# Sixteen slots for expert weights, earlier first loads, a router product with standing weights, and expert results added straight to the residual

## The reference, cut to what matters

```
x = x + g1 * y                                # y: the merged branches through w_o
u = modulate(rmsnorm(x, norm2_g), sh2, sc2)
logits = u @ router_w + router_b              # 256 x 32
top_val, top_idx = top_k(logits, 4); gate = softmax(top_val)
for each expert e, with the tokens that chose it (padded):
    hcat = u[tok] @ w1[e] + b1[e]             # 1024 -> 2048
    h_glu, h_lin = min(hcat[:, :1024], 7), clip(hcat[:, 1024:], -7, 7)
    act = h_glu * sigmoid(1.702 * h_glu) * (h_lin + 1)
    y_tok += gate * (act @ w2[e] + b2[e])     # 1024 -> 1024
x = x + g2 * y;  return rmsnorm(x, final_norm_g)
```

## Time and profile before

| | us |
|---|---|
| median of 3 runs | 2567.33 |
| profiled execution | 2567.04 |
| its span, first to last instruction | 2565.2 |
| first pass starts / last unit of the last pass ends | 1603.91 / 2544.28 |
| TensorE busy | 2408.0 (94%) |
| VectorE busy | 725.1 (28%) |
| ScalarE busy | 410.0 (16%) |
| HBM traffic | 604.65 MB read, 236 GB/s over the span |

### The profile page before, as it was taken

How to read it: one execution, slowest core, us unless ns; L and a number is a source line. 1 busy time by engine, 2 the same in 40 slices (tenths; PEclk the granted TensorE clock), 3 DMA queues, 4 the chain that set the end, 5 groups by cost and what they waited for, 6 DMA issues and landing times.

```text
span 2565.2 us, 32855 instructions
## 1 busy us (share of the span) xinstructions
PE 2408.0 (94%) x13468; PEld 1806.2 (70%) x13468; DVE 725.1 (28%) x1780; ACT 410.0 (16%) x928; POOL 0.2 (0%) x4
## 2 busy tenths in 40 slices
PE   8789998999889998999999898999999999999997
PEld 7678887888778887888876587555555555555554
DVE  6722264120432212000344543112111211111112
ACT  4222101000322102000023412111111111111111
POOL 0000000000000000000000000000000000000000
PEclk9899999999999999999999997999999999999999
DMA  6024475664214442132211054899999999999996
GB/s 248 33 99 152 160 276 189 240 226 170 81 66 140 156 148 115 66 115 91 71 70 49 7 211 184 359 422 421 422 422 422 421 422 421 422 421 422 421 422 261
DMA packets 83842, 606.90 MB, mean 237 GB/s; under 512 B 9328, under 2 KB 9712, under 8 KB 10000
## 3 DMA queue, kind: packets, MB, share of 16 engines
q1 hardware_dynamic: 83760, 605.73, 59.8%
HBM read 604.65 MB, written 1.05 MB: 236 GB/s over the span
## 4 chain that ended last, share of the span: by engine, by line
PE 79%; DMA 10%; DVE 7%; ACT 3%; issue 1%; SPq 0%; ACTq 0%; DVEq 0%
PE bank L521 30%; PE bank L898 13%; DMA spare<-in_experts 9%; PE bank L518 8%; PE bank L576 6%; PE bank L925 6%; PE bank L863 3%; PE bank L535 2%; PE bank L892 2%; DVE arena L1355 2%; PE bank L561 2%; PE bank L874 1%; PE bank L641 1%; DVE arena L1240 1%; ACT arena L1148 1%
## 5 line engine op out<-in xcount | busy, mean ns | idle before, releaser
L521 PE MATMUL bank<-arena,ring 128*128 128x256 f32 x3648 | 802.5, 383 | 24.5 <-DVE arena L1246 12.0
L521 PEld LDWEIGHTS bank<-arena,ring 128*128 128x128 f32 x3648 | 701.2, 193 | 124.6 <-issue 27.1
L898 PE MATMUL bank<-ring,arena 128*64 128x256 f32 x2304 | 293.8, 382 | 17.1 <-DMA ring<-in_experts 9.6
L898 PEld LDWEIGHTS bank<-ring,arena 128*64 128x64 f32 x2304 | 175.1, 137 | 130.9 <-DMA ring<-in_experts 19.0
L1703 DVE TENSOR_SCALAR arena<-bank 128x256 f32<-128x256 f32 x64 | 27.2, 425 | 703.6 <-PE bank L898 703.6
L518 PE MATMUL bank<-ring,arena 128*128 128x256 f32 x896 | 196.3, 381 | 0.0
L518 PEld LDWEIGHTS bank<-ring,arena 128*128 128x128 f32 x896 | 171.3, 191 | 23.6
L576 PE MATMUL bank<-arena,ring 128*128 128x256 f32 x704 | 152.3, 379 | 0.0
L576 PEld LDWEIGHTS bank<-arena,ring 128*128 128x128 f32 x704 | 133.8, 190 | 18.2
L1276 DVE SCALAR_TENSOR_TENSOR arena<-bank,par,arena 128x254 f32<-128x254 f32 (+1 forms) x176 | 72.7, 476 | 224.3 <-ACT arena L988 224.3
L898 PE MATMUL bank<-spare,arena 128*64 128x256 f32 x768 | 117.5, 382 | 7.9 <-DMA spare<-in_experts 7.9
(11 more groups left out here) (245 smaller groups left out, 1922.5 us busy)
## 6 DMA issues: line engine op xcount, KB each, us to landing
ring<-in_dense SPq DMA_DIRECT2D x186, 1024.0 KB, 4.8
ring<-in_experts SPq DMA_DIRECT2D x160, 1024.0 KB, 22.1
arena<-in_experts SPq DMA_DIRECT2D x128, 1024.0 KB, 21.4
spare<-in_experts SPq DMA_DIRECT2D x96, 1024.0 KB, 20.4
con<-in_con SPq DMA_DIRECT2D x1, 1248.0 KB, 12.1
X<-in_x SPq DMA_DIRECT2D x1, 1024.0 KB, 4.8
arena<-in_cond SPq DMA_DIRECT2D x1, 1024.0 KB, 17.7
arena<-in_ctx SPq DMA_DIRECT2D x1, 1024.0 KB, 4.8
```

Of the source, the lines that this page charges most:

```text
L521: ins = nc.tensor.matmul(o, w[:, k, j * P:(j + 1) * P], src[:, k, :], start=(k == 0), stop=(k == KT - 1))
L898: ins = nc.tensor.matmul(o, XGT[:, k, e * CAP:(e + 1) * CAP], w[:, k, :], start=False, stop=(k == KT - 1))
```

## The change

Slots. `EXPERT_RING` goes from 12 to 16. The working tiles of the passes move into the lower part of the arena (XGT, ACTT, GL, LN, SGM, SEL and SELG to columns 0 to 4095; YACC goes away), and the slots get ten places outside the ring, the five of the ring, and one more. Since 24 slabs are no multiple of 16, the hardware loop now runs 8 times over two passes (`body(p, odd)`), so each slab keeps a fixed slot in the program.

Loads. The wait for the end of the attention (`d_pv`) stands ahead of the second slab of `wb` instead of the first slab of `wa`. Behind it five expert slabs are issued, five more ahead of the first slab of `wo`, one after each of several waits, then five into the ring as it comes free, and one behind the last product.

Router. The product runs with the router weights standing (32 columns) and the tokens moving (256 columns), ahead of the turning of the tokens; ScalarE copies the 32 x 256 result out (LGT), TensorE turns it back to tokens x experts. VectorE then does both tiles of 128 tokens in each instruction. The selection for the first gather is made as soon as the places are there; the gates and the number of further rounds follow.

Biases b2. They lie in YE, with the gates in SGT, so the scatter of the first pass, which before spread zeros, brings them in. The product L852 and the copies L1668 go.

Results. `add_scattered` adds PSUM times the gate g2 to X itself, with eight instructions of 128x256 instead of four of 128x512 a pass, and the eight L1723 behind the last pass go. ScalarE loads the table for the square root before the last squares, and the output is stored in four pieces.

```diff
-EXPERT_RING = 12
+EXPERT_RING = 16
...
-            with eng.Fori(0 if first is None else first, PAIRS) as p:
-                body(p)
+            with eng.Fori(0 if first is None else first, PAIRS // 2) as m:
+                for odd in range(2):
+                    body(m * 2, odd)
...
-                if g == SLAB_AT["wa", 0]:
+                if g == SLAB_AT["wb", 1]:
                     sp.wait_ge(sem("d_pv"), HEADS)
+                    for j in range(5):
+                        first_load(j)
+                if g == SLAB_AT["wo", 0]:
+                    sp.wait_ge(sem("b_out"), KT)
+                    for j in range(5, 7):
+                        first_load(j)
+                    sp.wait_ge(sem("a_out"), KT)
+                    first_load(7)
+                    sp.wait_ge(sem("do_root"), 4)
+                    first_load(8)
+                    units_read(sp, "wa")
+                    first_load(9)
                     sp.dma_start(RW, d_routerw).then_inc(sem("routerw_in"), 16)
-                    sp.dma_start(B2, d_b2).then_inc(sem("b2_in"), 16)
+                if g == SLAB_AT["wo", 2]:
+                    sp.wait_ge(sem("ye"), 1)
+                    sp.dma_start(YE[0:EXPERTS, :], d_b2).then_inc(sem("b2_in"), 16)
...
+            for k in range(KT):
+                pe.wait_ge(sem("n10_h"), before("n10_h") + k + 1)
+                ins = nc.tensor.matmul(banks[0][0:EXPERTS, 0:T], RW[:, k, :], H[:, k, :], start=(k == 0), stop=(k == KT - 1))
+            ins.then_inc(sem("logits_t"), 1)
...
-            pe.wait_ge(sem("u2_out"), 4)
-            for c in range(KT):
-                ins = nc.tensor.matmul(acc(c), B2[:, c * P:(c + 1) * P], GTT, start=True, stop=True)
...
+            act.wait_ge(sem("logits_t"), 1)
+            nc.scalar.copy(LGT, banks[0][0:EXPERTS, 0:T]).then_inc(sem("lgt"), 1)
...
-                    V.tensor_tensor(YACC[:, 2 * j:2 * j + 2, :], YACC[:, 2 * j:2 * j + 2, :],
-                                    tiles(banks[6 + j % 2][:, :], 2), ALU.add).then_inc(sem("scat_read"), 1)
+                    for c in (2 * j, 2 * j + 1):
+                        ins = V.scalar_tensor_tensor(X[:, c, :], banks[6 + j % 2][:, c % 2 * T:(c % 2 + 1) * T],
+                                                     MOD[:, 40 + c, 0:1], X[:, c, :], ALU.mult, ALU.add)
+                    ins.then_inc(sem("scat_read"), 1)
...
-            for c in range(KT):
-                V.scalar_tensor_tensor(X[:, c, :], YACC[:, c, :], MOD[:, 40 + c, 0:1], X[:, c, :], ALU.mult, ALU.add)\
-                 .then_inc(sem("n11_x"), 1)
```

More of the change, by code:

```diff
@@ L406, in passes @@
             with eng.If(extra > 0):
-                with eng.Fori(PAIRS, (extra + 1) * PAIRS) as n:
-                    body(n)
+                with eng.Fori(PAIRS // 2, (extra + 1) * (PAIRS // 2)) as m:
+                    for odd in range(2):
+                        body(m * 2, odd)
         def total_pairs(eng):
@@ L844, in _ @@
-            pe.wait_ge(sem("gate_w"), 2)
+            for b in range(1, 4):
+                turn_tokens(b)
+            pe.wait_ge(sem("chosen"), 1)
+            M0 = SR[0][:, 0:32]
+            nc.tensor.matmul(banks[1][:, 0:64], C("before"), SR[0], start=True, stop=False, skip_group_check=True)
+            for to in (32, 64):
+                nc.tensor.matmul(banks[1][:, to:to + 32], ones, M0, start=False, stop=to == 32, skip_group_check=True)
+            nc.tensor.matmul(banks[1][:, 64:96], ones, SR[0][:, 32:64], start=False, stop=True, skip_group_check=True)\
+                .then_inc(sem("places"), 1)
@@ L1206, in sigmoid, with body @@
                 nc.scalar.activation(SGM[:, c % 2, :], GL[:, c % 2, :], ACT.Sigmoid, scale=1.702).then_inc(sem("sig"), 1)
-            def body(n):
+            def body(p, odd):
+                n = p + odd
                 sigmoid(n, 0)
@@ L1226, in _ @@
             passes(act, body)
-            square("n11", lambda c: X[:, c, :], "n11_x")
-            root("n11", 0)
+            n_end = total_pairs(act)
+            act.wait_ge(sem("n11_root"), before("n11_root"))
+            nc.scalar.activation(small[:, 121:122], EPS_COL, ACT.Sqrt)
+            for c in range(KT):
+                act.wait_ge(sem("scat_read"), n_end * 4 + (3 + c // 2))
+                nc.scalar.activation(SQ[:, c, :], X[:, c, :], ACT.Square).then_inc(sem("n11_sq"), 1)
+            act.wait_ge(sem("n11_sum"), before("n11_sum") + 1)
+            nc.scalar.activation(RS[:, 0:T], banks[STAT][:, 0:T], ACT.Sqrt, bias=EPS_COL).then_inc(sem("n11_root"), 1)
         @block.vector
```

267 lines of the change are left out of this document (136 added, 131 removed).

## The result

The changed kernel takes 2553.06 us in the median of 5 runs (2550.46 to 2556.89), the kernel before beside it 2568.29 (2567.14 to 2573.31, 5 runs): ratio 0.9938, 95% interval 0.9924 to 0.9953. It was timed again later beside other kernels: 2551.84, ratio 0.9928 (0.9915 to 0.9940). So it is faster, by 15 to 18 us (0.6 to 0.7%) and not by the 29 forecast, and it lies outside the range of 2532 to 2548.

A forecast was written before the change was run, and what follows sets the result against it. Full DMA engines were taken to bound the passes, at 59.69 us against TensorE's 57.02. Gains 2.4 + 12.0 + 9.9 + 4.9 = 29.2 us from 2567.04 gave 2537.8, taken as 2538; range 2532 to 2548.

The forecast's parts named there:

- Part 1: Start of `wa`: TensorE's 2.48 us wait for the first slab goes, 2.4 us gained (bounds 0 and 2.48).
- Part 2: From the router to the first pass: shorter router path and earlier gather, net 12.0 us gained (bounds 7 and 15.5).
- part 3: Expert passes: sixteen slots instead of 12 leave four slabs of 2.487 us less to load, 9.9 us gained.
- Neither wait behind it: Second `wb` and first `wo` slabs, behind early expert slabs: both arrivals forecast as covered by 16 us or more.
- the product at the full clock: Router product at 2.4 GHz takes half of 7.2 us: upper bound, 15.5 us gained up to the first pass.
- The cold gather of the rival: Gather ahead of the first pass stays at clock 0.50; cold-first-pass rival, 7 to 10 us gained instead of 12, chance 0.10.
- the cold first unit: Same cold-first-pass rival, chance 0.10: first unit also at clock 0.50, 7 us where the full clock gives about 3.5.
- The rival on code loading: TensorE's doubled loop body refetched at 7 jumps: 2540 to 2560 us, chance 0.05; over 6.3 us each, slower, 0.04.
- Part 4: Results added straight to X: about 0.22 us more a pass on TensorE, 3.5 in all, hidden in load waits, 0 net.
- Part 5: Tail after the last unit: earlier squares and root, smaller last store, 4.9 us gained (bounds 3 and 5.5).

The follow-up runs named there:

- the second profile: The changed kernel once more, unchanged, timed and profiled beside another kernel: 2551.84 us, ratio 0.9928 to the kernel before.
- the body moved by 120: The changed kernel with 120 additions to an unused semaphore at the start of TensorE's program: 2543.2 us, an estimate less the additions' 11.8 us.
- the written-out passes: The changed kernel with TensorE's 16 passes written out instead of a hardware loop of 8 x 2: 2549.65 us, ratio 0.9913.
- the body in place and the early mean: The changed kernel moved by 115 semaphore additions inside TensorE's waits, and without line 986's wait before the last norm's mean: 2539.48 us, ratio 0.9881.

## Why the prediction was wrong

It was right in direction, and wrong by 15 us in the time. The profiled execution missed its forecast of 2537.8 by 16.3 us: 11.0 in the passes, 5.7 ahead of `wa`, 3.0 in the tail, less 3.2 that parts 1 and 2 brought beyond their sums (to within 0.2). In the second profile, which has not the 5.7, it is 15.2 us, and the passes are 13.4 of them. So most of it is one step, part 3.

- **Part 1: right.** 2.6 us came (2.48 of them the wait), 2.4 were forecast. Neither wait behind it appeared.
- **Part 2: right in its mechanism, 3 us too low.** From the first instruction behind the statistics to the first pass it took 34.2 us and takes 19.2 (1591.88 - 1572.66): 15.0 us came instead of 12.0, close to the upper bound that I had for the product at the full clock. I read the 0.50 of the earlier trace rows on to a stretch that begins in another way; around the product without the turnings the window shows 0.91. The cold gather of the rival is there (5.95 us against 5.38), the cold first unit is not.
- **Part 3: wrong, and this is the step that failed.** I took 9.9 us; -1.1 came (-3.5 and -4.0 in two more profiles of the same passes). The step said that 16 slots spare four slabs of 2.487 us. They do where the code stays in place: with the body moved by 120 the stretch is 931.5, which is 8.9 us less than before. Here they paid for something that the sum held at nothing: the body's code is fetched in each iteration. That has two costs. First, half of the parts of every load fall behind, by 13 us at the end, and this alone eats the gain, as the written-out passes show (941.8 without any jump). Second, the jumps hold TensorE up by 23.5 us, against 15 us of waits that were there to hide them; alone they would cost some 8 of the 9.9, which is worked out and was not run by itself. The two do not add up: TensorE, held up at the jumps, comes late enough that it waits only 4.2 us for slabs.
- **The rival on code loading** named the cause and its sign (packets in the middle of the passes), at a chance of 0.05 for a few us a jump, and the measured time lies in the 2540 to 2560 that it gave. Its price counted the stop alone and left out the drop of the clock behind it, and what the packets do to the loads. It noted that 1640 instructions and the control instructions fit by little into the 2048 that the Trainium skill, "Runtime: NRT & Kernel Launch", section "Instruction fetch mechanics", gives for TensorE. The runs do not bear out that a loop has all of these: it is kept up to seven blocks of 256, counted from the start of the one in which it begins. That the trace of before held no packet said nothing about a body twice as long, and I should have weighed it at a half.
- **Part 4: right.** The waits for the first add rose from 7.2 to 10.3 us in all, 0.2 a pass, a part of the 57.2.
- **Part 5: mis-sized.** 1.9 instead of 4.9 us. I had overlooked the wait of line 986 (1.2 us) and that the mean takes TensorE 3.6 us behind the scatter (the root ends 0.9 us later than summed for it). The scatter started 0.7 us later than I had it, which stays open. The last 0.2 are small differences in the norm and the store. Adds and squares were sized rightly.
- **The profiled execution's 5.7 us** ahead of all this go with the lower clock in its first 50 us and belong to no step.

With the body in place and the early mean, which is not part of the change, the kernel takes 2539.48, where 2538 was forecast. That is partly luck: part 2 brought 3 us more than summed, the tail 1 less, and the passes 3 less.

## What to carry to other kernels

Before a loop body is lengthened, add up its instructions and where the loop begins, and compare the packets of instructions inside the loop in both profiles; here 50 to 120 instructions far ahead of the loop decided over 10 to 39 us. A resource that seems to be bound only by its rate (here the loads) can be held up by its slowest part, so look at how far the parts of one transfer land from each other. If a new cost is said to hide in waits that are there anyway, and the same change is to remove these waits, count both: what the waits can still hide, and what is left to gain.

## What the runs showed of the hardware that was not expected

- Where TensorE's instructions were fetched and the loads set the pace (420 GB/s), eight of the sixteen parts of each load fell behind the others: by 9 to 10 us over 700 us with 53 packets. With TensorE setting the pace they stayed together, within 1.0 to 1.5 us in the mean at a DMA share of 0.65 (56 packets) and 2.2 to 3.7 us at 410 GB/s (52 packets). That the packets ride on these eight is concluded from this; no row names the engine of a packet.
- A loop on TensorE was kept when its body, counted from the start of the packet in which it begins, ended at 1786 instructions or less, and was fetched in every iteration from 1836 on.
- A jump to code that isn't held cost TensorE 0.8 to 1.4 us at a DMA share of 0.65, 2.3 to 4.1 with full engines, and 4.8 to 9.0 when the next packet begins within the first 50 instructions behind the target. The granted clock was 0.50 in the 2 us window behind one such stop of the changed kernel. Why single jumps of one kernel differ by 1.6 us and more was not tried.
- An addition to a semaphore took TensorE 0.153 us at the start of the program (50, 60 and 120 of them put the first matmul at 8.57, 10.11 and 19.28 us). Ninety of them inside a wait of 10.7 us cost nothing, so there one took 0.12 us or less.
